# Sparse attention: scores packed in full banks, values and row sums as separate narrow matmuls

## The chip, the cores and the metric

The kernel runs on one core of one Trainium2 chip. The metric is the device time of one execution in microseconds (us), the median of several runs. A core has TensorE (PE in the profile, with its weight loads as PEld), VectorE (DVE), ScalarE (ACT), GpSimd (POOL) and SyncE (SP, which here issues DMAs), each with a queue worked off in order.

## The reference, cut to what matters

The program is a transformer of several layers on 512 tokens of width 1024. The change is in one part of it, the sparse attention of the second block: 16 query heads of 64 in 8 pairs, three branches a head (compressed keys; two branches over all 512 keys with a causal mask, which is what selection and window come to at this length), each with a softmax of its own, then a gate for each branch:

```python
s = einsum('q d, k d -> q k', q, k) * HEAD_DIM**-0.5
p = softmax(where(kpos <= qpos, s, -inf))        # per head and branch
o[b] = p @ v
out = g[0] * o[0] + g[1] * o[1] + g[2] * o[2]    # then @ w_out
```

## The kernel before, in words

The stage works with keys on partitions and queries along the row ("turned"). A pair p has 18 steps (STEPS, lines 139 and 140): for six BLOCKS (branch, half of the pair) one step for the compressed branch 0 and four steps (key tiles kt 0 to 3 of 128 keys, SEQ - 128 kt = 512, 384, 256, 128 queries) for branches 1 and 2. All queues are written out by hand; there is no planner.

- TensorE, `scores_turned`: two matmuls for the keys' high part and for the low part with the maxima (fp32r, L1743 and L1745), and between them a 128x128 causal square (L1744), into bank 0 or 2. Step i waits for the exponential of step i - 2.
- ScalarE, `exps`: the exponential of a step's bank into one of four homes PT (L2697); it waits until the value matmul of four steps before is done.
- TensorE, `outputs_turned`: three steps later (LAG) the value matmul of plain fp32 (L1774). Its 128 stationary columns are 64 of values and 64 of ones, in the order that puts the head's output into its half of the bank and the row sums into the other.
- ScalarE, `keep_outputs`: copies each finished bank; an odd head's copy and its sum are two instructions (L2719, L2723). SyncE sends each sum row to 16 partitions (L934), one transfer after the other.
- Beside it the maxima of the next pair: `find_max` (16 matmuls a pair of 512 to 128 columns, L1700, three banks) and `find_cmp_max` (L1713) on TensorE, `read_max` and `read_cmp_max` on VectorE, `turn_max` (L1721) and `max_to_rows`.
- The pair before is finished meanwhile: `shares` (gate over sum) on VectorE, two transfers by `shares_back`, `spread_share` (L1790) on TensorE, `weigh_parts` (three products, two adds) and `output_low` on VectorE, `output_parts` on ScalarE. The output projection follows (`late_chunks`, L1084); the last pair's spreads stand between its units.

The order of TensorE's queue is the loop behind `rope_part(11, 6, KC)`: scores, then maxima, then spreads, then values, in each step.

Of the kernel before, what the change touches and what calls it, by code (L numbers as in the profile page):

```python
# [19 lines left out]
ALU = mybir.AluOpType  # L20
# [118 lines left out]
BLOCKS = [(0, 0), (1, 0), (0, 1), (1, 1), (2, 0), (2, 1)]  # L139
STEPS = [(_x, _kt) for _x, (_b, _half) in enumerate(BLOCKS) for _kt in range(QT if _b else 1)]  # L140
LAST = [max(_i for _i, (_y, _kt) in enumerate(STEPS) if _y == _x) for _x in range(len(BLOCKS))]
MAXES = [(_t, _half, _b) for _t in reversed(range(QT)) for _half in range(2) for _b in (1, 2)]
N_STEPS, N_BLOCKS, N_MAXES = len(STEPS), len(BLOCKS), len(MAXES)
FINDS = [(0,), (1, 2), (3,), (4,), (5, 6), (7,), (8,), (9,), (10,), (11, 12, 13), (14, 15)]
FIRST_FINDS = [(), (2, 3), ()] + FINDS[3:]
LAG = 3
STACK = 4
TURN_AT, SPREADS_AT, ROWS_AT = 12, (11, 13, 14), (14, 15)
# [135 lines left out]
def build(nc, stream, experts, x_in, vecs_in, consts_in, invcnt_in, iota_in, out):  # L284
    with ExitStack() as ctx:
# [44 lines left out]
        WALK = sb("cell_walk", [P, 2, CELLS + 1], mybir.dt.int32)  # L330
        o_bytes, end_bytes = C * T1 * 4, 2 * FC * SEQ * 4 - C * T1 * 4
# [150 lines left out]
        PT = placed("probs_turned", x_at + 16 * KB, [P, 4, SEQ])  # L482
# [4 lines left out]
        PTR = placed("probs_turned_hi", x_at + 16 * KB, [P, 4, SEQ], F32R)  # L487
# [4 lines left out]
        ODDSUM = placed("odd_sums", ev_at + 12 * KB, [P, SEQ])  # L492
# [273 lines left out]
        def max_bank(n, x):  # L766
            return PS[:, (1, 3, 5, 7)[x % 4] if n == 0 else (1, 3, 7)[x % 3], :]
# [4 lines left out]
        def out_bank(p, x):  # L772
            return PS[:, (4, 6)[x % 2] if p + 1 < PAIRS2 else (4, 7, 6)[x % 3], :]

        def spread_bank(p, b):
            return PS[:, (5, 1, 3)[b], :]

        def o_part(p, b):
            return OP[:, BRANCHES * ((p + 1) % 2) + b, :]
# [48 lines left out]
        def _(sp):  # L828
# [96 lines left out]

            for p in range(PAIRS2):
                for x, (b, half) in enumerate(BLOCKS):
                    done = N_BLOCKS * p + x

                    sp.wait_ge(o_kept, done + 1)  # L930
                    if done:

                        sp.wait_ge(sum_moved, 16 * done)
                    sp.dma_start(SUMP[pieces(half, b), p % 2, :], ODDSUM[0:1, :] if half else o_part(p, b)[HD:HD + 1, :]).then_inc(sum_moved, 16)  # L934
                    if p and x == 0:
                        shares_back(p - 1)
# [57 lines left out]
        def _(pool):  # L994
# [34 lines left out]
            pool.memset(CHOOSE[:, :, :].bitcast(F32), 0.0).then_inc(forms_set, 1)  # L1029

# [43 lines left out]
        def _(pe):  # L1074
# [604 lines left out]
            def find_max(n, x):  # L1679

                t, half, b = MAXES[x]

                pe.wait_ge(qs_ready, 2 * n + half + 1)
                if n == 0 and x == 2:

                    pe.wait_ge(cmax_read, 1)
                if n == 0 and x >= 4:

                    pe.wait_ge(max_read, x - 3)
                if n:  # L1690

                    pe.wait_ge(max_read, N_MAXES * n + max(x - 2, 0))
                    if x == 2:

                        pe.wait_ge(max_rows, 2 * n)
                    if n > 2 and x < 2:

                        pe.wait_ge(part_ready, BRANCHES * (n - 2) - 1 + x)
                g = 2 * (n // 4) + half
                pe.matmul(max_bank(n, x)[:, 0:P * (t + 1)], QS[n][half][:, P * t:P * (t + 1)], KS1[:, b - 1, g, 0:P * (t + 1)],  # L1700
                          start=True, stop=True).then_inc(max_done, 1)

            def find_cmp_max(n):

                pe.wait_ge(qs_ready, 2 * n + 2)
                if n > 2:

                    pe.wait_ge(part_ready, BRANCHES * (n - 2) - 2)
# [7 lines left out]
            def turn_max(n):  # L1716

                pe.wait_ge(max_read, N_MAXES * (n + 1))
                pe.wait_ge(cmax_read, n + 1)
                for t in range(QT):  # L1720
                    mm = pe.transpose(PS[:, 7, t * P:(t + 1) * P], MAXT[:, t, :], ident)  # L1721
                mm.then_inc(max_turned, 1)

            def scores_turned(p, i):

                x, kt = STEPS[i]
                b, half = BLOCKS[x]
# [7 lines left out]
                q0, s = P * kt, score_bank(i)  # L1735
                qs, qm = QS[p][half][:, q0:SEQ], QM[p][half][:, q0:SEQ]
                if b == 0:
                    first, second = (k[:, half, p // 4, :, :].rearrange("p b n -> p (b n)") for k in (KC1, KC2))
                    pe.matmul(s, first, qs, start=True, stop=False, skip_group_check=True)
                    pe.matmul(s, second, qm, start=False, stop=True, skip_group_check=True).then_inc(st_done, 1)  # L1740
                    return
                g = 2 * (p // 4) + half
                pe.matmul(s[:, 0:SEQ - q0], KS1[:, b - 1, g, q0:q0 + P], qs, start=True, stop=False, skip_group_check=True)  # L1743
                pe.matmul(s[:, 0:P], CAUR[:, :], IDA[:, :], start=False, stop=False, skip_group_check=True)  # L1744
                pe.matmul(s[:, 0:SEQ - q0], KS2[:, b - 1, g, q0:q0 + P], qm, start=False, stop=True, skip_group_check=True).then_inc(st_done, 1)  # L1745

            def outputs_turned(p, i):

                x, kt = STEPS[i]
                b, half = BLOCKS[x]  # L1750
                done = N_BLOCKS * p + x

                if b == 0:
                    pe.wait_ge(cmp_low, 2 * p + half + 1)
                else:
                    pe.wait_ge(exp_done, N_STEPS * p + i + 1)
                if p == 0 and x == 0:

                    pe.wait_ge(ones_set, 5)
                if kt == 0 and p + 1 == PAIRS2 and x == 1:  # L1760

                    pe.wait_ge(max_rows, 2 * PAIRS2)
                elif kt == 0 and p + 1 == PAIRS2 and x > 1:

                    pe.wait_ge(o_kept, done - 2)
                elif kt == 0 and done >= 2:

                    pe.wait_ge(o_kept, done - 1)
                probs = PT[:, (N_STEPS * p + i) % 4, 0:SEQ - P * kt]
                if b == 0:  # L1770
                    mm = pe.matmul(out_bank(p, x)[:, :], VCS[:, p // 4, half * HD:half * HD + P], PTR[:, (N_STEPS * p + i) % 4, :], start=True, stop=True,
                                   skip_group_check=True)
                else:
                    mm = pe.matmul(out_bank(p, x)[:, P * kt:SEQ], VV[:, b - 1, p // 4, kt, half * HD:half * HD + P], probs, start=kt == 0,  # L1774
                                   stop=kt == QT - 1, skip_group_check=True)
                mm.then_inc(pv_done, 1)

            def spread_share(p, b):

                pe.wait_ge(share_moved, 32 * (p + 1))  # L1780
                if p and b == 0:

                    pe.wait_ge(part_ready, BRANCHES * p)
                if b == 0:

                    pe.wait_ge(cmax_read, min(p + 3, PAIRS2))
                else:

                    pe.wait_ge(max_read, N_MAXES * min(p + 3, PAIRS2))
# [27 lines left out]
            first_maxima(8, 12)  # L1817
            rope_part(10, 4, KC)
            first_maxima(12, N_MAXES)
# [10 lines left out]
            for p in range(PAIRS2):  # L1830
                for i in range(N_STEPS):
                    scores_turned(p, i)
                    if p + 1 < PAIRS2:
                        if p and i == 0:
                            find_cmp_max(p + 1)
                        for x in (FINDS if p else FIRST_FINDS)[i] if i < len(FINDS) else ():
# [3 lines left out]
                    if p and i in SPREADS_AT:  # L1840
                        spread_share(p - 1, SPREADS_AT.index(i))
                    if i >= LAG:
                        outputs_turned(p, i - LAG)
                    elif p:
                        outputs_turned(p - 1, N_STEPS + i - LAG)
            for i in range(N_STEPS - LAG, N_STEPS):
                outputs_turned(PAIRS2 - 1, i)

            def late_chunks(c, first, last):

                n, r = U["wo2"] + c, R["wo2"] + c
                if r % PAIRS >= 2:

                    pe.wait_ge(o_kept, PAIRS2 * N_BLOCKS)
# [10 lines left out]
            for c in range(AHEAD, C):  # L1865
                n, r = U["wo2"] + c, R["wo2"] + c
                pe.wait_ge(o_kept, PAIRS2 * N_BLOCKS)
# [157 lines left out]
        def _(act):  # L2025
# [615 lines left out]
            def max_to_rows(n, half):  # L2641

                act.wait_ge(max_turned, n + 1)
                act.activation(QM[n][half][other_rows(half), :], PS[other_rows(half), 7, :], ACT.Copy, scale=-1.0).then_inc(max_rows, 1)
# [34 lines left out]
            def exps(p, i):  # L2679

                x, kt = STEPS[i]
                step = N_STEPS * p + i
                b, half = BLOCKS[x]
                width = SEQ - P * kt

                act.wait_ge(st_done, step + 1)
                if step >= 4:

                    act.wait_ge(pv_done, step - 3)
                if b == 0:  # L2690
                    act.activation(PTR[:, step % 4, :], score_bank(i), ACT.Exp)
                    if p or half:

                        act.wait_ge(cmp_low, 2 * p + half)
                    act.activation(CEX[HD:P, :], score_bank(i)[HD:P, :], ACT.Exp).then_inc(exp_done, 1)
                    return
                act.activation(PT[:, step % 4, 0:width], score_bank(i)[:, 0:width], ACT.Exp).then_inc(exp_done, 1)  # L2697

            def keep_outputs(p, x):

                b, half = BLOCKS[x]
# [1611 lines left out]
```

## Time and profile before

| | |
|---|---|
| median of 3 runs | 1941.61 us (1941.1 to 1942.29) |
| profiled execution, its own time | 1941.49 us |
| its span | 1939.7 us |
| PE / PEld busy | 1919.9 us (99%) / 1559.4 us (80%) |
| DVE / ACT / POOL busy | 1385.9 us (71%) / 975.8 us (50%) / 28.7 us (1%) |
| costliest group of the stage | L1774, 256 records, 90.9 us |

The span runs from the first to the last instruction. Busy is the time in which an engine has an instruction in work; matmuls are pipelined, so the lengths of their records overlap, and only the pieces of the chain of waits add up.

### The profile page before, as it was taken

The numbers are of one execution on the slowest core, as the hardware profiler recorded it, in microseconds if no ns is written. First come the engines' busy times: TensorE is split into PE (matmuls) and PEld (weight loads), VectorE is DVE, ScalarE is ACT, GpSimd is POOL, SyncE is SP. The second block draws the span as 40 slices with busy tenths as digits, with TensorE's granted clock in tenths as the row PEclk, the third lists the DMA queues.
The fourth block names the chain that finished last, engine by engine and source line by source line (L and its number), as shares of the span: only waits on it lengthen the run. The fifth ranks groups of instructions, "written<-read, shape, count | busy, mean of one in ns | idle before, by whom it ended". The sixth has DMA issues, their size and how long they took to land.

```text
span 1939.7 us, 26815 instructions
## 1 busy us (share of the span) xinstructions
PE 1919.9 (99%) x9038; PEld 1559.4 (80%) x9038; DVE 1385.9 (71%) x2195; ACT 975.8 (50%) x1422; POOL 28.7 (1%) x50
## 2 busy tenths in 40 slices
PE   9999999999999999999999999999999999999998
PEld 9987888887777788878778888888886788888887
DVE  7986444566999875867746888863388778888534
ACT  5656433446778533677765333333366543333322
POOL 0000000001000000000000000000011000000000
PEclk9999999999999999999999999999999999999999
DMA  5220333326999435400003333333341133333332
GB/s 193 88 66 12 98 97 97 97 94 224 359 350 357 168 89 159 135 23 3 3 6 116 97 95 94 95 103 100 108 123 47 46 97 97 97 97 96 99 108 88
DMA packets 69115, 219.41 MB, mean 113 GB/s; under 512 B 12128, under 2 KB 15360, under 8 KB 68896
## 3 DMA queue, kind: packets, MB, share of 16 engines
q1 hardware_dynamic: 64720, 212.46, 33.7%
q10 hardware_dynamic: 4304, 5.77, 1.2%
q8 instruction: 53, 0.87, 0.2%
q14 instruction: 38, 0.31, 0.1%
HBM read 209.05 MB, written 2.10 MB: 109 GB/s over the span
## 4 chain that ended last, share of the span: by engine, by line
PE 90%; DVE 6%; ACT 2%; issue 1%; DMA 0%; ACTq 0%; SPq 0%; DVEq 0%
PE psum L1084 61%; PE psum L1580 7%; PE psum L1774 3%; PE psum L1554 2%; PE psum L1599 1%; PE psum L1491 1%; PE psum L1563 1%; PE psum L1745 1%; PE psum L1252 1%; PE psum L1700 1%; PE psum L1924 1%; PE psum L1743 1%; PE psum L1634 1%; DVE w_lo L2944 1%; DVE sig L3219 1%
## 5 line engine op out<-in xcount | busy, mean ns | idle before, releaser
L1084 PE MATMUL psum<-x_hi,w_hi 128*128 128x512 f32 (+1 forms) x1344 | 494.1, 378 | 0.0
L1084 PE MATMUL psum<-x_hi,w_lo 128*128 128x512 f32 (+1 forms) x1344 | 490.1, 375 | 0.0
L1084 PE MATMUL psum<-x_lo,w_hi 128*128 128x512 f32 (+1 forms) x1344 | 490.0, 375 | 0.0
L2944 DVE TENSOR_TENSOR w_lo<-raw,w_hi 128x1024 fp32r<-128x1024 f32 x243 | 296.3, 1220 | 187.5 <-ACT w_hi L2046 187.1
L2046 ACT ACTIVATE w_hi<-raw 128x1024 fp32r<-128x1024 f32 x243 | 256.2, 1055 | 190.2 <-DMA raw<-stream 189.5
L1084 PEld LDWEIGHTS psum<-x_hi,w_hi 128*128 128x128 f32 x1344 | 246.5, 188 | 47.3 <-issue 1.9
L1084 PEld LDWEIGHTS psum<-x_lo,w_hi 128*128 128x128 f32 x1344 | 246.5, 188 | 46.5 <-issue 1.4
L1084 PEld LDWEIGHTS psum<-x_hi,w_lo 128*128 128x128 f32 x1344 | 246.4, 188 | 45.5
L1084 PE MATMUL psum<-hid_hi,w_hi 128*128 128x512 f32 (+2 forms) x710 | 261.0, 375 | 0.5 <-DVE hid_lo L4126 0.5
L1084 PE MATMUL psum<-hid_hi,w_lo 128*128 128x512 f32 (+2 forms) x710 | 259.7, 373 | 0.0
L1084 PE MATMUL psum<-hid_lo,w_hi 128*128 128x512 f32 (+2 forms) x710 | 259.6, 373 | 0.0
L2063 ACT ACTIVATE staged<-psum 128x512 f32<-128x512 f32 (+1 forms) x116 | 69.1, 595 | 216.6 <-PE psum L1084 202.4
L1084 PEld LDWEIGHTS psum<-hid_hi,w_hi 128*128 128x128 f32 x710 | 131.4, 188 | 25.4 <-issue 1.1
L1084 PEld LDWEIGHTS psum<-hid_hi,w_lo 128*128 128x128 f32 x710 | 131.3, 188 | 23.5
L1084 PEld LDWEIGHTS psum<-hid_lo,w_hi 128*128 128x128 f32 x710 | 131.3, 188 | 23.5 <-issue 0.2
L2169 ACT ACTIVATE squares<-squares 128x512 f32<-128x512 f32 x44 | 27.9, 633 | 215.0 <-DVE squares L3095 215.0
L1774 PE MATMUL psum<-probs_turned,values_and_ones 128*128 128x512 f32 (+3 forms) x256 | 90.9, 438 | 0.0
L3035 DVE TENSOR_TENSOR resid<-resid,staged 128x512 f32<-128x512 f32 x39 | 26.9, 689 | 79.3 <-ACT staged L2063 77.4
L2931 DVE TENSOR_TENSOR w_lo_more<-raw_more,w_hi_more 128x1024 fp32r<-128x1024 f32 x56 | 67.0, 1212 | 12.1 <-ACT w_hi_more L2033 12.1
L3821 DVE CUSTOM_DVE_ANT_0 psum<-psum,causal_mask 128x512 f32<-128x512 f32 (+3 forms) x128 | 60.3, 514 | 12.2 <-PE psum L1700 11.7
L2931 DVE TENSOR_TENSOR w_lo<-raw,w_hi 128x1024 fp32r<-128x1024 f32 x57 | 68.1, 1211 | 0.7 <-ACT w_hi L2033 0.7
L2697 ACT ACTIVATE probs_turned<-psum 128x512 f32<-128x512 f32 (+3 forms) x128 | 55.0, 431 | 25.9 <-PE psum L1745 24.4
(651 smaller groups left out, 2966.6 us busy)
## 6 DMA issues: line engine op xcount, KB each, us to landing
raw<-stream SPq DMA_DIRECT2D x251, 512.0 KB, 3.6
raw<-experts SPq DMA_DIRECT2D x70, 512.0 KB, 5.3
raw_more<-experts SPq DMA_DIRECT2D x68, 512.0 KB, 5.3
staged<-staged ACTq DMA_DIRECT2D x64, 64.0 KB, 3.2
out_fm<-resid SPq DMA_DIRECT2D x7, 256.0 KB, 2.2
resid<-x_fm SPq DMA_DIRECT2D x3, 528.0 KB, 7.3
consts<-consts_in SPq DMA_DIRECT2D x1, 1373.0 KB, 14.1
staged<-staged SPq DMA_DIRECT2D x20, 64.0 KB, 2.7
```

The lines of the kernel that those rows point to most:

```text
L1084: last = pe.matmul(o, wt[:, slot, k * P:(k + 1) * P], m[part], start=start and p == 0, stop=stop and p == 2, skip_group_check=True)
L1554: mm = pe.matmul(pair(r)[:, half, :], HT[:, b, :] if m % M_OUT == 0 else HTW[:, :], moe_slot("raw", s)[:, half * 512:(half + 1) * 512], st ...
L1580: mm = pe.matmul(pair(r)[:, 0, :], x[:, part, f * P:(f + 1) * P], moe_slot(kind, s)[:, k * 512:(k + 1) * 512], start=f == 0 and p == 0, st ...
L1774: mm = pe.matmul(out_bank(p, x)[:, P * kt:SEQ], VV[:, b - 1, p // 4, kt, half * HD:half * HD + P], probs, start=kt == 0, stop=kt == QT - 1 ...
L2046: act.activation(w_hi[:, slot, :], raw[:, slot, :], ACT.Copy).then_inc(hi_split, 1)
L2063: act.activation(shaped(dst, t), result(rslot, t), func, **more).then_inc(lin_free, 1)
L2169: act.activation(SQ[:, j, 0:T2], SQ[:, j, 0:T2], ACT.Silu).then_inc(act_done, 1)
L2697: act.activation(PT[:, step % 4, 0:width], score_bank(i)[:, 0:width], ACT.Exp).then_inc(exp_done, 1)
L2931: dve.tensor_tensor(moe_slot("lo", s), moe_slot("raw", s), moe_slot("hi", s).bitcast(F32), ALU.subtract).then_inc(m_ready, 1)
L2944: dve.tensor_tensor(w_lo[:, slot, :], raw[:, slot, :], w_hi[:, slot, :].bitcast(F32), ALU.subtract)\
L3035: dve.tensor_tensor(h, h, staged(E0[name] + c, t), ALU.add).then_inc(ev_used, 1)
L3821: dve.tensor_tensor_reduce(out=s, in0=s, in1=AFTER[:, SEQ - width:], scale=1.0, scalar=NEG, op0=ALU.add, op1=ALU.max, accum_out=MAXT[:, t, ...
```

## The change

A pair has 12 steps, each a full bank of 512 columns: two for the compressed branch, four for key tile 0, four that hold key tile 1 (384) and key tile 3 (128) of one branch and head, two that hold key tile 2 (256) of both heads. Two parts in a bank share one causal matmul of 256 columns. Maxima of query tile 1 take both branches in one matmul, those of tile 0 lie four in a bank; their banks are two instead of three. Probabilities have eight homes. Values are computed in three bursts a pair (`values_side_by_side`): key tile 0 after step 8, tiles 3 and 1 after step 11, tile 2 in step 1 of the next pair. Each value matmul has 64 stationary columns, and the two heads of a branch go to partitions 0 to 63 and 64 to 127 of one bank; the sums are matmuls of their own with 32 columns of ones, four to a bank. ScalarE keeps two full banks and one bank of sums; the sums go out in four transfers at once. The two adds a pair go to GpSimd (all but the last pair's), and the third spread and product of a pair move to the pair after the next.

```diff
+STEPS = [[(0, _half, 0, 0)] for _half in range(2)] + [[(_b, _half, 0, 0)] for _b, _half in ROW] \
+    + [[(_b, _half, 1, 0), (_b, _half, 3, SEQ - P)] for _b, _half in ROW] + [[(_b, _half, 2, SEQ // 2 * _half) for _half in range(2)] for _b in (1, 2)]
+VALUES = [[0], [3, 1], [2]]
+SLOTS_PT, STACK = 8, 4
+FINDS = [(), (0,), (1,), (2, 3), (4,), (5, 6), (7,), (8,), (9,), (10,), (), ()]
+CMP_AT, TURN_AT, ROWS_AT = 1, 10, (10, 11)
+CMP_OUT_AT, VALUES_AT = (3, 4), (8, 11, 1)
+SPREADS_AT, LAST_SPREADS_AT = (10, 11, 0), (8, 9, 10)
...
+            def sums_out(p):
+                sp.wait_ge(o_kept, N_KEPT * (p + 1))
...
+                for x, (b, half) in enumerate(ROW):
+                    sp.dma_start(SUMP[pieces(half, b), p % 2, :], SUMR[32 * x:32 * x + 1, :]).then_inc(sum_moved, 16)
...
+            def add_parts(p):
+                for b in (1, 2):
+                    pool.wait_ge(part_ready, BRANCHES * p + b + 1)
...
+                    pool.tensor_tensor(o_part(p, 0), o_part(p, 0), o_part(p, b), ALU.add).then_inc(parts_added, 1)
...
+                    pe.wait_ge(max_read, N_MAXES * n + max(x - 1, 0))
...
+                for x, (b, half, kt, col) in enumerate(STEPS[i]):
+                    pe.matmul(s[:, col:col + SEQ - P * kt], KS1[...], QS[p][half][:, P * kt:SEQ], start=x == 0, stop=False, ...)
+                if len(STEPS[i]) == 1:
+                    pe.matmul(s[:, 0:P], CAUR[:, :], IDA[:, :], ...)
                 else:
+                    squares = s.rearrange("p (c n) -> p c n", n=P)[:, 0:QT:STEPS[i][1][3] // P, :]
+                    pe.matmul(squares, CAUR[:, :], IDA[:, :].unsqueeze(1).to_broadcast([P, 2, P]), ...)
...
+            def values_side_by_side(p, x):
+                pe.wait_ge(exp_done, N_STEPS * p + VALUES_NEED[x])
...
+                for b in (1, 2):
+                    for kt in VALUES[x]:
+                        for half in range(2):
+                            i, col = PLACE[b, half, kt]
+                            pe.matmul(values_bank(b)[half * HD:(half + 1) * HD, P * kt:SEQ], VV[:, b - 1, p // 4, kt, 2 * half * HD:(2 * half + 1) * HD],
+                                      PT[slot_of(p, i)][:, col:col + SEQ - P * kt], start=kt == 0, stop=kt == 2, skip_group_check=True)
+                for kt in VALUES[x]:
+                    for row, (b, half) in enumerate(ROW):
+                        i, col = PLACE[b, half, kt]
+                        mm = pe.matmul(sums_bank()[32 * row:32 * row + 32, P * kt:SEQ], VV[:, b - 1, p // 4, kt, HD:HD + 32],
+                                       PT[slot_of(p, i)][:, col:col + SEQ - P * kt], start=kt == 0, stop=kt == 2, skip_group_check=True)
+                mm.then_inc(pv_done, 1)
...
             for p in range(PAIRS2):
                 for i in range(N_STEPS):
                     scores_turned(p, i)
+                    if i == SPREADS_AT[2] and 2 <= p:
+                        spread_share(p - 2, 2)
+                    if i == VALUES_AT[2] and p:
+                        values_side_by_side(p - 1, 2)
                     if p + 1 < PAIRS2:
+                        if p and i == CMP_AT:
                             find_cmp_max(p + 1)
+                        for x in (FINDS if p else FIRST_FINDS)[i]:
                             find_max(p + 1, x)
                         if i == TURN_AT:
                             turn_max(p + 1)
+                    if i in CMP_OUT_AT:
+                        cmp_outputs(p, CMP_OUT_AT.index(i))
...
+                    if i in VALUES_AT[0:2]:
+                        values_side_by_side(p, VALUES_AT.index(i))
...
 # ScalarE, in each step after exps(p, i)
+                    if p and i in (1, 2):
+                        keep_values(p - 1, i)
+                    if p and i == 3:
+                        keep_sums(p - 1)
+                    if i == 4:
+                        keep_cmp(p, 0)
+                    if i == 5 and p + 2 < PAIRS2:
                         queries_high(p + 2)
+                    if i == 6:
+                        keep_cmp(p, 1)
+                    if i == 7 and p > 1:
+                        output_parts(p - 2)
...
 # VectorE, in each pair
                 if p > 1:
+                    weigh_part(p - 2, 2)
+                cmp_probs_low(p, 0)
                 if p and p + 1 < PAIRS2:
                     read_cmp_max(p + 1)
                     read_max(p + 1, 0)
+                    read_max(p + 1, 1)
...
+                cmp_probs_low(p, 1)
...
+                    for x in range(2, 7):
+                        read_max(p + 1, x)
                 if p:
                     shares(p - 1)
                 if p + 1 < PAIRS2:
+                    for x in range(7, N_MAXES):
                         read_max(p + 1, x)
```

## Rows read from the trace of the kernel before

**Rows 1.** The page: busy time by engine, and the chain by engine.

```profile
PE 1919.9 (99%) x9038; PEld 1559.4 (80%) x9038; DVE 1385.9 (71%) x2195; ACT 975.8 (50%) x1422; POOL 28.7 (1%) x50
PE 90%; DVE 6%; ACT 2%; issue 1%; DMA 0%; ACTq 0%; SPq 0%; DVEq 0%
```

**Rows 2.** Stretches: us, busy of PE, PEld, DVE, ACT, POOL, clock, DMA, GB/s.

```profile
828.80:1000.70 171.90, 170.77 (x896) 133.71 (x895) 120.50 (x342) 137.11 (x280) 0.89 (x2) 1.00 0.04 8
...
893.96:915.83 21.87, 21.87 (x120) 17.46 (x119) 16.31 (x49) 17.67 (x36) 0.00 (x0) 1.00 0.02 2
```

**Rows 3.** The chain of waits over one pair, 893.6 to 915.45: start, us, piece.

```profile
by line: PE psum L1774 40.4%; PE psum L1745 14.6%; PE psum L1700 13.7%; PE psum L1743 10.7%; PE psum L1744 5.3%; PE psum L1713 3.6%; PE psum L1790 3.4%; PE psum L1739 3.1%; PE psum L1740 2.1%; PE psum L1771 2.1%; PE psum L1721 2.0%
...
894.00 0.80 PE psum L1713 x8
...
895.12 0.65 PE psum L1774 x2
895.76 0.23 PE psum L1743
895.99 0.06 PE psum L1744
896.05 0.29 PE psum L1745
...
897.94 0.22 PE psum L1774 x2
...
898.92 0.06 PE psum L1743
898.98 0.11 PE psum L1744
899.09 0.11 PE psum L1745
...
904.89 0.48 PE psum L1700 x3
905.37 0.93 PE psum L1774 x2
```

**Rows 4.** The chain at matmuls of small shapes: fox values, compressed values.

```profile
138.57 0.32 PE psum L1252 x2
138.89 0.32 PE psum L1236
...
755.99 1.02 PE psum L1675 x16
757.00 1.12 PE psum L1084 x4
```

**Rows 5.** ScalarE's groups, 850 to 980 us: busy, mean ns; idle before, releaser.

```profile
L2697 ACT ACTIVATE probs_turned<-psum 128x512 f32<-128x512 f32 x24 | 14.4, 598 | 11.2 <-PE psum L1745 10.9
...
L2723 ACT ACTIVATE odd_sums<-psum 1x512 f32<-1x512 f32 x18 | 10.6, 587 | 0.2
L2715 ACT ACTIVATE o_parts<-psum 128x512 f32<-128x512 f32 x18 | 10.5, 584 | 0.0
```

**Rows 6.** VectorE's groups, 850 to 980 us, and GpSimd's, whole span.

```profile
L3821 DVE CUSTOM_DVE_ANT_0 psum<-psum,causal_mask 128x512 f32<-128x512 f32 x24 | 16.4, 704 | 0.2
...
L3897 DVE TENSOR_TENSOR o_parts<-o_parts 128x512 f32<-128x512 f32 x12 | 8.3, 692 | 0.4
...
L3872 DVE RECIPROCAL gate_over_sum<-sum_pieces 96x32 f32<-96x32 f32 x6 | 2.1, 344 | 0.0
...
L1024 POOL TENSOR_TENSOR cmp_values_stacked<-cmp_values_and_ones,cmp_values_stacked 31x384 fp32r<-31x384 f32 x2 | 2.8, 1380 | 119.7 <-ACT cmp_values_stacked L2668 119.6
```

**Rows 7.** L934, the sums' transfers: issue ns, and time to landing.

```profile
L934 SPq DMA_DIRECT2D sum_pieces<-odd_sums x24: 502/502/565, 841.8 to 1002.4; - x24
...
DMA to landing us min/median/max: 1.6/1.6/3.4
```

More of the change, by code:

```diff
@@ L481, in build @@
         QM = [lo_pair("q_and_max_first", 2)] + [qm_ring[n % 2] for n in range(PAIRS2 - 1)]
-        PT = placed("probs_turned", x_at + 16 * KB, [P, 4, SEQ])
+        homes = [x_at + (16 + 2 * n) * KB for n in range(4)] + [x_at + (32 + 2 * n) * KB for n in range(2)] + [more_at + 2 * n * KB for n in range(2)]
+        PT = [placed(f"probs_turned_{n}", home, [P, SEQ]) for n, home in enumerate(homes)]
         SUMP = placed("sum_pieces", x_at + 24 * KB, [P, 2, PIECE])
@@ L1679, in find_max @@
             def find_max(n, x):
-                t, half, b = MAXES[x]
-                pe.wait_ge(qs_ready, 2 * n + half + 1)
+                t, half, bs = MAXES[x]
+                pe.wait_ge(qs_ready, 2 * n + (1 if half is None else half) + 1)
                 if n == 0 and x == 2:
@@ new lines, in scores_turned, with cmp_outputs @@
+                for b, half, kt, col in STEPS[i]:
+                    mm = pe.matmul(s[:, col:col + SEQ - P * kt], KS2[:, b - 1, 2 * (p // 4) + half, P * kt:P * (kt + 1)], QM[p][half][:, P * kt:SEQ],
+                                   start=False, stop=True, skip_group_check=True)
+                mm.then_inc(st_done, 1)
+            def cmp_outputs(p, half):
+                pe.wait_ge(cmp_low, 2 * p + half + 1)
+                if p == 0 and half == 0:
+                    pe.wait_ge(ones_set, 5)
+                if p:
+                    pe.wait_ge(o_kept, N_KEPT * (p - 1) + 3 + half)
+                pe.matmul(out_bank(half), VCS[:, p // 4, half * HD:half * HD + P], PTR[slot_of(p, half)][:, :], start=True, stop=True,
+                          skip_group_check=True).then_inc(pv_done, 1)
@@ L2679, in exps @@
             def exps(p, i):
-                x, kt = STEPS[i]
                 step = N_STEPS * p + i
-                b, half = BLOCKS[x]
-                width = SEQ - P * kt
                 act.wait_ge(st_done, step + 1)
[L2687 to L2694, printed above, removed]
+                if step >= SLOTS_PT:
+                    q, j = divmod(step - SLOTS_PT, N_STEPS)
+                    act.wait_ge(pv_done, N_OUTS * q + FREES[j])
@@ L3936, in _ @@
                     dve.tensor_tensor(CHOOSE[0:2 * SUMS2, :, :].rearrange("p b (h d) -> p h b d", h=2), hi_rows, lo_rows, ALU.add)
+                elif p + 1 < PAIRS2:
+                    for b in range(2):
+                        weigh_part(p - 1, b)
+                else:
+                    for b in range(BRANCHES):
+                        weigh_part(p - 1, b)
             for n in range(2, AHEAD + 1):
@@ L3940, in _ @@
             shares(PAIRS2 - 1)
-            weigh_parts(PAIRS2 - 1)
+            for b in range(BRANCHES):
+                weigh_part(PAIRS2 - 1, b)
+            add_parts(PAIRS2 - 1)
             output_low(PAIRS2 - 1)
```

296 lines of the change are left out of this document (147 added, 149 removed).

## The prediction

> **What bounds the kernel now.** The page comes first: TensorE is busy for 99% of the span and holds 90% of the chain that ended last [rows 1]. Its stretches come next, at a granted clock of 1.00: the sparse attention lies at 828.8 to 1000.7 us, 171.9 us for eight pairs of heads, and one middle pair takes 21.87 us, in which TensorE is busy for all 21.87, ScalarE for 17.67, VectorE for 16.31 and GpSimd not at all [rows 2]. Then the chain inside a pair, where each piece on TensorE is the time until the next may go: it splits the pair completely [rows 3]. L1774 (values) has 40.4% of it, 8.84 us; the turned scores (L1743 to L1745) 30.6%; the maxima (L1700) 13.7%. The stage is bound by TensorE's columns, with nothing of another engine to be seen between them. What is to be read is therefore how many columns TensorE streams, what short matmuls waste, and whether the new order lets another engine into the chain.
>
> **The values.** A value matmul is plain fp32 and leaves two records: 512 columns take 0.93 us, against 0.23 for a score matmul of 512, so it is four passes, two in each record; 384 take 0.65 and 128 take 0.22 [rows 3]. Before, a pair has 16 of them (4 sets of 512, 384, 256 and 128), 8.84 us. Their 128 stationary columns are 64 of values and 64 of ones. The change issues each twice: with 64 columns of values, the two heads in the two halves of one bank, and with 32 columns of ones, four in the four quarters of another. Nothing in this trace shows two matmuls in different columns of the array at once, so the price is bounded from both sides. If they share no time, 32 matmuls of these lengths cost 2 x 8.84 = 17.68 us. If neighbours run wholly beside each other, two heads cost one and four sums cost one: 8.84/2 + 8.84/4 = 6.63. I take 6.63: the outputs lie in disjoint partitions, the weights in disjoint columns, the order in the code alternates between them, and no data orders them. The Trainium skill, TensorEngine Tiling (Array Packing), Tiling Modes, states that different tiles load weights and multiply in parallel; no run here shows it.
>
> **Changing the shape of the array.** Each of a pair's three bursts of values goes from 128 columns to 64, to 32, and back: 9 changes a pair. The nearest rows are matmuls of small shapes [rows 4]. The fox value of 16 rows and 16 columns takes 0.32 us where its columns need under 0.05, and the 272 columns behind it 0.32 where 272/512 of 0.23 is 0.12: 0.45 for two changes. Sixteen records at L1675, 31 stationary columns and 64 moving, two passes each, take 1.02 where their columns need 16 x 0.23/4 = 0.92 or less, and the four matmuls of 512 behind take 1.12 for 4 x 0.23 = 0.92: about 0.3 for two changes. So a change costs 0.1 to 0.23. The value taken is 0.15 (nearest to L1675, which is narrow in columns as here): 9 x 0.15 = 1.35 a pair, bounds 0.9 and 2.1. The same page of the Trainium skill, Key Properties, says that changing the mode drains TensorE, and the rows agree: 0.3 to 0.45 us for a way in and out.
>
> **Scores and maxima.** Their columns stay the same (5120 twice, 2048 of causal squares, 5120 of maxima). What goes is the wait for weights behind a matmul of 128 columns: the matmul of 512 behind the square takes 0.29 instead of 0.23, and the two behind a short key matmul 0.11 each where 0.06 would do [rows 3]. Steps 1+3 share a square of 256 columns, and so do the two halves of step 2: about 0.07 less for each of 4 double banks and 0.1 for 2, 0.5 a pair. Of the 16 maxima eight short ones become four of 256 and 512 columns: three short ones take 0.48 [rows 3], so 0.25 less. Together 0.75 a pair, bounds 0.4 and 1.0.
>
> **ScalarE, VectorE and GpSimd.** ScalarE evacuates ten full banks (6.0 us at 598 ns) instead of 16 partial ones (6.9), and keeps six outputs instead of nine (about 0.59 each) [rows 5]: 17.7 falls to about 15. VectorE gives two adds of 0.69 a pair to GpSimd; it reads the same columns of maxima. GpSimd's two-input operation of 384 columns takes 1.38 [rows 6], so 1.84 for 512 and 3.7 a pair, beside some 21 us in which it has nothing else: no cost on the path. If it slows VectorE, the whole overlap is 3.7 us a pair and VectorE has over 5 idle; bounds 0 and 0.5.
>
> **The new order puts waits in.** Values now come in three bursts, so between the third burst (in the next pair's second step) and the first burst (ninth step) TensorE does seven steps of scores without values to cover the others: pieces as above give 0.80 (compressed maxima) + 4.4 (scores: four banks at 0.58, three at 0.69) + 1.9 (nine maxima) + 0.46 (two compressed outputs), about 7.5 us up to the tenth maximum. That matmul waits for reads that stand on VectorE behind the shares of the pair before. Those need all six sums: ScalarE reaches the sums after two exponentials and two kept banks, at about 1.8 + 4 x 0.6 = 4.2 us; SyncE then issues four transfers at 0.5, each 1.6 to landing [rows 7], so the last lands at about 7.3; reciprocal and its followers take about 1.0 (0.34 for the first), a read 0.7 [rows 6]: 9.0. The maximum, and the first burst queued behind it, come up to 1.5 us late. ScalarE is a second limit: the ninth scores want the seventh exponential, the last of some ten operations of 0.6 that start at 1.8, so at about 7.8. I take 1.0 for six of the eight pairs (the first has no shares behind it, the last no maxima), bounds 0 and 2.0. Eight homes hide the rest: an exponential wants the home of eight steps before, which the matching burst has left by then.
>
> **Tail.** Before, the chain goes from the values straight into the output projection, and the three spreads at 1010.3 cost 0.2 of waiting. After, the four transfers go together instead of one after another and are as early: 0, bounds -0.5 and 1.5.
>
> **The sum.** A pair: values 6.63 - 8.84 = -2.21; changes +1.35; short matmuls -0.75: -1.61. Eight pairs: -12.9; stalls 6 x 1.0 = +6: -6.9 us. The profiled run before took 1941.49, 1.8 more than its span of 1939.7 and 0.1 under the median of 1941.61. That gives 1934.6, told as 1935. This case's own range: cheap changes (0.9), best savings (1.0) and no stall give 8 x -2.31 = -18, so 1923; dear ones (2.1, 0.4, 2.0 in six pairs) 8 x 0.29 + 12 = +14, which I don't expect together: 1947.
>
> **Rivals.**
> - **Two records in order (slower).** Each fp32 value matmul is two records on the same columns of the array. If matmuls start in the order issued, the second record of one waits for its first, and only this second record can run beside the next matmul's first. Then every matmul costs one record's time whether two or four stand side by side: 32 x half of before = 8.84 a pair, plus the first record of each of six groups alone (0.47, 0.06 and 0.22, twice, about 1.5): 10.3 instead of 6.63, 3.7 more, 8 x 3.7 = 30: 1965. For it: the two records that each L1774 row counts. Against: nothing here. It decides whenever a queued record blocks the one behind it. TensorE: Matmul & The Clock Gate (the Trainium skill), Part 3, has matmuls start and end strictly in program order, which is this mechanism; no run here shows it yet. Between (half of the overlap lost) lies 1950.
> - **No overlap at all.** 17.68 instead of 6.63: 8 x 11.05 = 88 us: 2023. Against: the disjoint columns. It is also the case in which the change doesn't do what it says.
> - **Overlap, but the stalls eat it (no change).** Changes at 0.2 (+0.45 a pair) and stalls of 1.5 (+0.5 in six): +6.6 on 1935: 1941. For: the walk above gave up to 1.5. Against: the kept slack of 5 us on both engines.
> - **Overlap and free stalls.** 1923, as above.
>
> **Chances.** Overlap as forecast or better 0.47 (1923 to 1937); overlap with stalls 0.13 (1937 to 1947); records in order 0.30 (1950 to 1975); none 0.10. About 0.2% (3.9 us) is what a measurement of this kernel can tell from no change. Faster by more 0.46, within it 0.13, slower 0.41. The range, 1921 to 1968, takes in all but the worst of the third case and the fourth.
>
> **What would show it.** Right: in the chain, values plus sums near 6.6 us a pair, a pair of 20.3 us, and idle time before the tenth maximum released by VectorE. Value records of both heads starting together would show overlap; starts one whole record apart would show the order rival; sums as dear as values would too. GpSimd at 3.7 us a pair, beside an unchanged VectorE row. Wrong: a pair over 22 us with TensorE never idle (order, or no overlap), or TensorE idle over 2 us a pair.

## The result and the profile after

The changed kernel takes 1966.18 us (median of 4 runs, 1962.33 to 1972.3) against 1941.45 (1941.1 to 1942.29) of the kernel before on the same chip: a ratio of 1.0119, interval 1.0099 to 1.0138. It is slower by 1.2%. The forecast was 1935, and 1966 lies inside the range only because the order rival (1965) widened it. As will be seen, that rival's mechanism is not what happened. Some executions of several kernels here, the one before too, take 5 to 6 us longer than the rest (in the profiled ones of e3, e7 and e7b TensorE ran at half clock for 13.65 us from 411 us on, far ahead of the sparse attention), which lifts the median of e7b, where half of them do, by some 2 us.

The page of the kernel after, busy time by engine and the chain by engine (against [rows 1]):

```profile
PE 1919.4 (98%) x9214; PEld 1531.2 (78%) x9214; DVE 1382.1 (70%) x2181; ACT 956.2 (49%) x1350; POOL 47.4 (2%) x64
PE 89%; DVE 5%; ACT 2%; DMA 1%; issue 1%; SPq 1%; DVEq 0%; ACTq 0%
```

TensorE's busy time is the same 1919 us although the values should have become cheaper, and DMA and SyncE's queue have entered the chain with 1% each, 10 to 29 us apiece (the page rounds). Where the sparse attention ends tells where all of it lies: 1000.72 us before, 1024.37 after, which is 23.65 later, and the span grew by 23.6. Stretches of the kernel after (columns as in [rows 2]): the whole stage to 1026, then ten us and ten more in its last pair.

```profile
828.80:1026.00 197.20, 171.27 (x1078) 106.07 (x1079) 115.26 (x325) 118.03 (x208) 18.67 (x14) 0.96 0.03 7
1003.00:1013.00 10.00, 3.15 (x15) 1.84 (x15) 2.28 (x6) 3.93 (x7) 0.00 (x0) 0.70 0.03 4
1013.00:1023.00 10.00, 10.00 (x67) 4.28 (x65) 4.34 (x4) 2.52 (x4) 3.36 (x2) 0.78 0.00 0
```

Reading the start of each pair's compressed scores in both traces gives the account of the 23.65 us: 0.8 before the second pair, then 1.3, 1.7, 1.7, 1.7, 4.3 and 1.7 for six middle pairs, and 10.5 for the last. A quiet middle pair, one at a granted clock of 1.00 throughout, takes 23.54 us (897.30 to 920.84) against 21.87, and TensorE is busy for 21.37 of it where before it never stopped [rows 2]. The pair with 4.3 (944.38 to 970.61) is not quiet: the landing of its sums takes 2.78 us instead of 1.73, and its first burst 3.55 instead of 1.94, with the clock at half for 3.41 us from 959.31.

The chain inside that pair, against [rows 3], up to and through its first burst, then its second and third:

```profile
902.67 0.35 ACT o_parts L2790
...
903.15 0.60 ACT probs_turned L2762
903.75 0.50 ACT sum_rows L2798
...
904.27 0.57 SPq L957
...
904.89 0.58 SPq L957
...
905.52 0.58 SPq L957
...
906.14 1.73 DMA sum_pieces<-sum_rows
...
907.89 0.02 SPq L964
...
907.94 1.64 DMA sum_pieces<-o_parts
...
909.66 0.35 ACT o_parts L2778
...
910.27 0.60 ACT cmp_probs_turned L2779
910.86 0.14 issue
911.00 1.94 PE psum L1831 x8
912.93 1.00 PE psum L1836 x8
913.93 0.43 PE psum L1797 x2
...
916.26 0.65 PE psum L1777 x4
...
917.97 1.88 PE psum L1831 x16
919.84 1.00 PE psum L1836 x16
...
922.20 1.01 PE psum L1831 x8
923.22 0.57 PE psum L1836 x8
```

Two things are to be seen. The bursts (the three groups of value and sum matmuls of a pair) are cheap: L1831 (values) and L1836 (sums) take 2.94 + 2.88 + 1.58 = 7.40 us a pair where L1774 took 8.84. And ahead of the first one stands a chain without TensorE: ScalarE keeps the four sums (L2798), SyncE issues their transfers (L957), the last one lands, only then (L964) does SyncE send the compressed sum of the even head, that lands, ScalarE may overwrite its source (L2778, L2779), and only then may the burst overwrite the bank they were read from. In the last pair the same chain is followed by the shares on their way back (L948, then the spread L1852), and by a slow burst:

```profile
1006.92 0.60 ACT cmp_probs_turned L2779
...
1007.54 0.50 SPq L965
...
1008.14 0.78 SPq L948
...
1008.96 2.07 DMA share_rows<-gate_over_sum_parts
...
1011.07 0.80 PE psum L1852
1011.87 3.61 PE psum L1831 x8
1015.48 1.87 PE psum L1836 x8
```

The burst that took 1.94 + 1.00 takes 3.61 + 1.87: half speed, the lower of the clock's two levels (1.2 GHz), granted from 1007.09 to 1017.33. From 1003.07 to 1011.07, ahead of the burst, TensorE had been busy for 1.16 of 8 us. The shares' way back is not new in this place. The last pair of the kernel before has it too, with TensorE busy for 6.57 of the 6.75 us from 985.63 to 992.38:

```profile
989.41 0.78 SPq L924
...
990.24 2.10 DMA share_rows<-gate_over_sum_parts
```

### The profile page after: what moved, and what is told of

Its sections match the earlier page's. It is cut to its first block, busy times and chain, and to the rows that moved or that the text cites. A ratio compares the mean times of both kernels' runs of the same rounds, so it can differ in the third digit from the quotient of the medians.

```text
span 1963.3 us, 26958 instructions
## 1 busy us (share of the span) xinstructions
PE 1919.4 (98%) x9214; PEld 1531.2 (78%) x9214; DVE 1382.1 (70%) x2181; ACT 956.2 (49%) x1350; POOL 47.4 (2%) x64
## 4 chain that ended last, share of the span: by engine, by line
PE 89%; DVE 5%; ACT 2%; DMA 1%; issue 1%; SPq 1%; DVEq 0%; ACTq 0%
PE psum L1134 63%; PE psum L1630 6%; PE psum L1604 2%; PE psum L1831 2%; PE psum L1649 1%; PE psum L1541 1%; PE psum L1613 1%; PE psum L1302 1%; PE psum L1836 1%; PE psum L1991 1%; PE psum L1684 1%; DVE sig L3300 1%; DVE psum L4102 1%; DVE psum L3905 1%; DMA sum_pieces<-sum_rows 0%
## 5 line engine op out<-in xcount | busy, mean ns | idle before, releaser
L3905 DVE CUSTOM_DVE_ANT_0 psum<-psum,causal_mask 128x512 f32<-128x512 f32 (+3 forms) x128 | 60.1, 514 | 33.7 <-PE psum L1752 29.8
L2762 ACT ACTIVATE probs_turned<-psum 128x512 f32<-128x512 f32 x80 | 47.3, 594 | 38.0 <-PE psum L1805 36.9
L3170 DVE TENSOR_TENSOR staged<-psum,scratch 128x512 f32<-128x512 f32 x88 | 60.3, 686 | 5.8 <-PE psum L1134 4.8
```

What stands on the lines that cost most here:

```text
L2762: act.activation(PT[slot_of(p, i)][:, :], score_bank(i), ACT.Exp).then_inc(exp_done, 1)
L3170: dve.tensor_tensor(EV[:, slot, 2:2 + T2], PS[:, 2 * ((r0 + m) % PAIRS), :], TS[:, 2, 0:T2], ALU.mult)\
L3905: ins = dve.tensor_tensor_reduce(out=s, in0=s, in1=AFTER[:, SEQ - width:], scale=1.0, scalar=NEG, op0=ALU.add, op1=ALU.max, accum_out=MAXT ...
```

## Experiments

Lines are two lower from e1 on, except in g1, which has the changed kernel's, and p1 and e6, where some differ again: L1829 and L1834 are the changed kernel's L1831 and L1836, L1748 and L1750 its L1750 and L1752, L1767 its L1769, L3903 its L3905. All are timed beside the kernel before on the same chip (its medians: 1941.91 for the first four, 1942.11 for the next four, 1941.75 for the three after, 1941.63 for the last). A ratio is not exactly the quotient of the two medians. A pair's length is that of a middle pair in the chain of the profiled execution.

**The compressed sums counted by themselves (e1).** The even head's compressed sum waited for the landing of the four other sums only because all six share one semaphore.

```
-  sp.wait_ge(sum_moved, 16 * (N_SUMS * p + half))       # behind the four others
+  sp.wait_ge(gates_moved, 16 * (PAIRS2 + 2 * p + half)) # a count of its own
```

> The changed kernel with one edit: the transfers of the compressed sums are counted on a count of their own, so that the even head's compressed sum no longer waits until the four sums of the pair before have landed. Theory A (waits): the value bursts overlap fully and cost 7.4 us a pair, and the time is lost before the first burst of each pair, in a chain sums kept, four issues, landing (1.73), compressed sum, landing (1.64), odd output kept. One landing leaves the chain; then the shares on VectorE (behind the same landing, about 1.0, and a read of 0.7) are late next, so about 1.1 of the 1.7 comes back in seven pairs: 8 us less than the changed kernel, about 1958. Theory B (shape of the array): narrow matmuls and the changes between them cost what the pair lost, and the waits only fill it: no change, 1966.

1957.09 us, ratio 1.0096 (1.0067 to 1.0125), a pair of 22.86 us. The landing left the chain and 9.5 us came back by the medians (each against the kernel before beside it), 7.8 between the two profiled executions, so this chain was real. It held 0.7 us in most pairs, 2.0 of the last pair (28.18 us for 30.20), and the 2.7 us that one pair lost more than the others. What stands ahead of the first burst in e1's middle pairs is VectorE's reads and split and ScalarE's copies of the queries, not the shares, which I had expected next.

**Compressed output kept and sent ahead of the sums (e2 = e1 and this; SyncE's order and count follow).**

```
-  if p and i == 3: keep_sums(p - 1)
-  if i == 4: keep_cmp(p, 0)
+  if i == 3: keep_cmp(p, 0)
+  if p and i == 3: keep_sums(p - 1)
```

> As e1_own_count, and the even head's compressed output is kept, and its sum sent, before the four sums of the pair before. Theory A: the whole chain over the compressed sum is gone, but the tenth maximum still stands behind the shares, so little more than e1_own_count comes back: 1953 to 1958. Theory B: no change, 1966. If theory A is right but the shares are not the next limit, 1945.

1963.51, ratio 1.0120 (1.0103 to 1.0137), a pair of 23.9: worse than e1, against my expectation. In its chain the sums are kept at 905.55, their last transfer lands at 910.66, and the shares and the reads queued behind them on VectorE hold the maxima. That is the stall that the prediction had walked, at last in the place it was given.

**Shares later on VectorE (e3 = e2 and this)**: two more reads of maxima ahead of them, the last pair's spreads a step later, the split of the odd compressed probabilities ahead of the two weight splits.

```
-  for x in range(2, 7): read_max(p + 1, x)
+  for x in range(2, 9): read_max(p + 1, x)
   shares(p - 1)
-  LAST_SPREADS_AT = (8, 9, 10)
+  LAST_SPREADS_AT = (9, 10, 11)
```

> As e2_cmp_first, and on VectorE two more reads of maxima stand ahead of the shares of the pair before; in the last pair the three spreads are one step later (behind the first burst), and the odd compressed probabilities are split before the two weight splits. Theory A: the first burst then waits only for ScalarE's exponentials, 2.3 us a pair earlier than in the changed kernel, and the last pair, which waited some 7 us for its shares, loses about 4: 1942 to 1947. Theory B: 1966 less the last pair's wait, about 1960.

1951.21, ratio 1.0048 (1.0031 to 1.0065), a pair of 22.86: 12 us better than e2 and still short of what I expected; ahead of the turned maxima (L1775) four reads of VectorE stood in the chain. The middle pair is only back at e1's 22.86; against e1 the 6 us are those of the last pair (22.04 us for 28.18).

**The last maxima a step earlier (e4 = e3 and this).**

```
-  FINDS = [..., (8,), (9,), (10,), (), ()]
+  FINDS = [..., (8,), (9, 10), (), (), ()]
```

> As e3_shares_later, and the last group of maxima (four short reads on VectorE, 1.2 us, for which the turning of the maxima waited) is computed one step earlier, ahead of the first burst. Theory A: this 1.2 us a pair hides beside the burst: 8 us less than e3_shares_later, 1934 to 1939, which would be under the kernel before (1941.5). Theory B: no change against e3_shares_later.

1944.38, ratio 1.0016 (1.0006 to 1.0026), a pair of 21.85. That is 6.8 us less than e3 where I expected 8, and outside the 1934 to 1939 that I had counted from a better e3. The wait before the turn has gone. Of the 24.7 us of loss, 22 are undone by one count and the order of the work, without touching the bursts.

**Order of issue, and twice as many changes of shape (g1 = the changed kernel and this)**: first burst head by head, second burst in four parts instead of two.

```
-  x == 0: for b: for half: matmul          # even, odd, even, odd
+  x == 0: for half: for b: matmul          # even, even, odd, odd
-  x == 1: values of blocks 3, 1; sums of blocks 3, 1
+  x == 1: values of 3; sums of 3; values of 1; sums of 1
```

> The changed kernel with two edits inside its bursts. First burst (key tile 0): the two value matmuls of the even heads, then the two of the odd heads, instead of alternating. If TensorE starts matmuls strictly in the order issued and each waits for its own columns, only the second and third can share time: 3 lengths of 0.86 instead of 2, so about 2.8 us instead of 1.94. If each set of columns has a queue of its own, 1.94 as before. Second burst: values of key tile 3, its sums, values of tile 1, its sums, so that the array's shape changes four times inside it instead of once and twice at its ends as before, two changes more. By my price (0.15 a change) the burst grows by 0.3 from 2.88 us; by the rival's (the changes are what the time went to) by 0.5 or more.

1963.16 in its one run. The chain of g1, first burst and second:

```profile
887.08 1.94 PE psum L1831 x8
889.03 1.00 PE psum L1836 x8
...
894.07 0.59 PE psum L1831 x8
894.65 0.36 PE psum L1836 x8
895.01 1.44 PE psum L1831 x8
896.45 0.78 PE psum L1836 x8
```

The first burst takes 1.94 and 1.00 in either order: two matmuls of the same columns in a row do not keep the other columns waiting. (A record doesn't say which columns it ran on; the burst's length and the records' starts, two at a time in both orders, say this.) The second takes 3.17 in four parts where it took 2.88 in two: 0.29 for two more changes, 0.15 each.

**The adds back on VectorE (p1 = e4 and this).**

```
-  pool: add_parts(p)        # two adds a pair
+  dve:  add_parts(p - 2), add_parts(p - 1) behind their products
```

> e4_maxima_earlier with the two adds of a pair back on VectorE, ahead of the compressed probabilities of the pair after the next. If GpSimd's adds cost nothing there, VectorE's 1.4 us stand in the chain that now ends the waits (maxima read, then found): up to 1.4 us in each of six pairs slower, 1949 to 1953 against 1944. If instead GpSimd's adds slowed VectorE beside them, no change or up to 3 us faster.

1944.08, ratio 1.0007 (0.9994 to 1.0020): the same as e4. The groups of 850 to 980 us show what GpSimd's adds do to VectorE; first the changed kernel (e4's mean is 1065), then p1 (the split of the compressed probabilities):

```profile
L3968 DVE TENSOR_TENSOR probs_turned_hi<-cmp_probs_turned,probs_turned_hi 64x512 fp32r<-64x512 f32 x12 | 12.8, 1066 | 5.8 <-ACT cmp_probs_turned L2760 5.7
```

```profile
L3965 DVE TENSOR_TENSOR probs_turned_hi<-cmp_probs_turned,probs_turned_hi 64x512 fp32r<-64x512 f32 x12 | 8.3, 689 | 7.2 <-ACT cmp_probs_turned L2756 6.9
```

Five of the twelve splits in this stretch run beside an add and take 1.59 or 1.60 us, the others 0.69, which makes the mean of 1066 ns: 0.9 us that VectorE loses in a pair, against 1.4 us of adds that it is spared.

**ScalarE's copies moved beside the bursts (e5 = e4 and this)**: the copy of the next queries from step 5 to 8, the odd compressed output from step 4 to 5, the second split behind two more reads.

```
-  if i == 5 and p + 2 < PAIRS2: queries_high(p + 2)
+  if i == 8 and p + 2 < PAIRS2: queries_high(p + 2)
-  CMP_OUT_AT = (3, 4)
+  CMP_OUT_AT = (3, 5)
```

> e4_maxima_earlier with ScalarE's two copies of the queries (0.63 each) after the ninth exponential, beside the first burst, instead of after the sixth, and VectorE's split of the odd compressed probabilities after the fourth read instead of after the second (its compressed output one step later). What is left in e4's chain before the first burst is VectorE's read and split (0.7 each) and ScalarE's copies, about 3 us of waits a pair. Theory A: 1.0 to 1.5 us of them go in six or seven pairs: 1935 to 1938, faster than the kernel before (1941.9). Theory B (full pairs are at TensorE's limit already): no change, 1944.

1944.27, ratio 1.0015 (1.0001 to 1.0028), the pair unchanged at 21.85: no gain, where I expected 6 to 9 us. ScalarE has left the chain, and what stands there instead is one engine, from the end of the compressed maxima's matmuls (L1767) to the fifth maximum. Chain of e5:

```profile
896.01 1.01 PE psum L1767 x8
...
897.04 0.43 DVE psum L3887
...
897.84 0.69 DVE psum L3903
...
900.67 0.69 DVE probs_turned_hi L3967
...
901.39 0.57 DVE psum L3903
...
902.21 0.41 PE psum L1748
```

VectorE's 5.2 us between 897.04 and 902.21 cannot start before the third burst and the compressed maxima are over: TensorE's chain of 16.6 and VectorE's of 5.2 make 21.8.

**The last pair's spreads behind its second burst (e6 = e5 and this).**

```
-  if p + 1 == PAIRS2 and i in LAST_SPREADS_AT: spread_share(p - 1, ...)   # before the burst
+  if p + 1 == PAIRS2 and i == N_STEPS - 1: all three spreads              # behind it
```

> As e5_copies_in_burst, and in the last pair all three spreads stand behind the second burst, since they waited 3 us for the shares' landing ahead of it. Theory A: about 2 us less, 1933 to 1936, unless the output projection then waits for the next to last pair's output (up to 1.5 us given back).

1944.68, ratio 1.0009 (0.9995 to 1.0024), no gain either. The burst no longer waits for the shares, but the products and the splits of the output weights now stand in the chain ahead of the output projection (3.7 us of L3024). The wait moved by one place.

**The third burst behind the maxima (e7 = e5 and this; e7b = e4 and this; e8 = e5 with it one step later still).**

```
-  step 1: scores, values(p - 1, 2), find_cmp_max, find 0
+  step 1: scores, find_cmp_max, find 0, values(p - 1, 2)
```

> e5 with the third burst of values (block kt=2, 1.6 us) issued after the compressed maxima and the first maxima matmul of the same step instead of ahead of them. In e5's trace VectorE stands in the chain from 897.04 to 902.21 (5.2 us: compressed maxima and five reads), and TensorE waits about 1.2 us in it for banks of maxima; the burst ends just ahead of it. Theory A (that chain of reads, begun behind the burst, is what holds e5 at the old 21.85 us a pair): the burst now lies beside the reads, the waits go, a pair takes 20.7 us, six pairs gain 1.1 each: 1937 us (1935 to 1940), under the kernel before. Rival B (the wait only moves: values are kept 1 us later, or the bank of the compressed maxima is not free yet because the third spread and its product stand in front): pair 21.8, 1944. Rival C (TensorE's own work fills the pair, records hide it): no change, 1944.

> As e7, but the third burst one step later still, behind the second maxima matmul of step 2, and ScalarE keeps the values one step later each (steps 2 and 3). Theory A: the reads' chain starts as early as in e7 and the burst sits in the middle of it, where e5's TensorE idles longest: 1936 (1934 to 1940). Rival B (values and sums are kept 1 us later, the transfers and the compressed probabilities behind them on ScalarE too): a wait ahead of the first burst of each pair, 1942 to 1950.

> The same edit as e7 on e4 (without e5's three moves). It tells whether e5's moves, worth nothing by themselves (1944.27 against 1944.38), matter once the maxima start earlier. Theory A: 1937 to 1941, no better than e7. If e5's moves are worth nothing in any case, both are equal; if e4 had a wait behind the reads (ScalarE's copy of the queries ahead of the odd compressed output), e7b stays 2 to 4 us above e7.

In the order of these texts, 1945.83 (e7; ratio 1.0026, 1.0015 to 1.0037), 1946.12 (e8; 1.0022, 1.0014 to 1.0031) and 1947.89 (e7b; 1.0027, 1.0016 to 1.0038): in all three theory A missed, by 6 to 7 us beyond its upper bound. The pair did not get shorter but longer, 22.25 in e7. In its chain the compressed maxima wait 0.86 us for the last product of the pair before, and behind the burst the third maximum is only issued at 905.03, so VectorE's reads begin again from there: 3.5 us of VectorE in a pair of 22.25.

**The whole chain of maxima earlier (e9 = e7 and this).**

```
-  FINDS = [(), (0,), (1,), (2, 3), (4,), (5, 6), (7,), ...]
+  FINDS = [(), (0, 1), (2,), (3, 4), (5,), (6,), (7,), ...]
-  step 0: scores, spread(p - 2, 2)
+  step 0: spread(p - 2, 2), scores
```

> e7 left the third maxima matmul where it was (step 3, 905.03 in its trace), behind the burst that it had put in front: VectorE read two maxima by then and waited, so the four reads and the split of 2.1 us stood in the chain after all, and the compressed maxima waited 0.84 us for the last product of the pair before. Here the maxima matmuls come one step earlier each (two of them beside the compressed maxima), and the third spread goes ahead of the compressed scores. Theory A (what keeps every rearrangement at the old 21.85 us a pair is VectorE's serial chain: compressed maxima, reads, split): with the chain begun earlier and the burst beside it a pair takes 20.8 to 21.2 us, 1938 us (1935 to 1941). Rival B (VectorE is late again in another place, since its product for the third spread now stands in front of the first split): 1943 to 1948.

1941.38 us, ratio 0.9996 (0.9986 to 1.0006): 3 us short of the 1938 that I expected, the best order found, and level with the kernel before. Its chain over the same part of the pair, and the stretch that holds five pairs and more:

```profile
894.69 0.97 PE psum L1767 x8
895.65 0.56 PE psum L1748 x2
896.22 1.01 PE psum L1829 x8
897.23 0.57 PE psum L1834 x8
...
901.17 0.57 DVE psum L3903
```

```profile
850.00:980.00 130.00, 126.90 (x856) 81.46 (x854) 89.08 (x273) 90.14 (x161) 14.02 (x12) 1.00 0.02 3
```

The burst lies beside VectorE's reads and one read is left in the chain. A pair takes 21.37 us, and adding up the chain's pieces over one (893.75 to 915.12) gives TensorE 20.28, VectorE 0.66 and 0.42 of issue. What this saves in six pairs (3.2 us) is given back at the ends. The second pair starts 1.3 us later than before, and the last takes 21.2 us (979.17 to 1000.36), 1.5 more than the last before: ahead of the shares' way back, which stood in the chain before too, the copy of the four sums, their issue and their landing stand in it now (984.85 to 989.31). The late start goes with the clock. In the first pair of e9, as of every kernel here with the new order except g1, TensorE runs at half clock for 3.41 us, which before it didn't; the stretch 828 to 836 ahead of it, in which it was busy for 3.38 of 8 us, had 7.70 before:

```profile
828.00:836.00 8.00, 3.38 (x15) 1.95 (x13) 6.13 (x14) 3.95 (x7) 0.85 (x2) 1.00 0.40 106
836.49:839.90 3.41, 3.41 (x12) 3.02 (x12) 1.36 (x6) 1.50 (x3) 0.00 (x0) 0.50 0.08 15
```

Half of 3.41 is 1.7, an estimate of what this costs, and enough for the 1.3.

## Why the prediction was wrong

- **Full overlap: right.** Two heads cost one, four sums cost one. Less the changes of shape, the first burst's four values cost 2 x 0.93 = 1.86 [rows 3] where the sets' rows show 1.94, and its four sums 0.93 where they show 1.00. In the trace the first two value records start within 0.01 us of each other at 911.00, and the first four of the sums within 0.02 at 912.86; g1 shows that the order of issue does not matter. The order rival (1965) and the one without overlap (2023) are wrong, the first in spite of its number.
- **0.15 us a change of shape: right.** g1 gives 0.29 for two. In the chain part of the cost sits in the piece behind each burst (L1797: 0.43 at 913.93, where undisturbed 384 and 128 columns take 0.23), so reading the bursts alone understates it: 7.33 in them and 3 x 0.2 behind make 7.93 a pair in e9, 1.30 over full overlap, for which the prediction had 1.35.
- **TensorE's own sum, -1.61 us a pair: right.** It asked for a pair of 20.3 us. e9's chain has 20.28 on TensorE against 21.87 before, -1.59. Less the 7.93 of values and 8.84 before, that leaves -0.68 for the short matmuls, for which the prediction had -0.75.
- **"Up to 1.5 us late", 1.0 taken, 2.0 the bound: this step failed.** The changed kernel loses 23.54 - 20.28 = 3.26 us in a quiet middle pair. The walk followed the four sums through the shares to the tenth maximum. Its times were good: it had the last sum land 7.3 us behind the third burst, the trace has 7.6 (900.24 to 907.88). But the path that it followed from there isn't in the chain. It left out that SyncE sends the compressed sum behind the same count, so behind the landing of the four (two transfers in a row, 1.73 and 1.64), that ScalarE's two copies of the odd compressed output wait for that, and that the first burst wants their bank. e1, which takes that one wait away, gives 9.5 us back. The walked stall itself shows only in e2, whose order makes it, and goes again in e3. The 13 us from e1 to e4 are the last pair's (6) and, at 1.0 us in each middle pair, four reads ahead of the turned maxima.
- **A second limit was not seen at all.** The prediction walked TensorE's steps against ScalarE and SyncE, and took VectorE's 5 idle us a pair for slack. But the compressed maxima, five reads and a split (5.2 us) are a serial chain. It starts when the third burst is over, and at its end TensorE waits for a bank to hold its next maximum. With the old values TensorE had enough to do meanwhile. That is why e5 stands at 21.85 us although TensorE's own work is 20.3 (in e4 ScalarE's copies of the queries stood in the chain too, behind three of these reads and the split). Only e9, which starts that chain ahead of the burst and has each maximum ready for it, comes under it.
- **Tail 0, bounds -0.5 and 1.5: wrong.** The last pair costs 10.5 us more. The same chain stands in it, and behind it the shares' way back (2.9 us from L948's issue to the spread), which the kernel before had under cover of a busy TensorE. From 995.49 to 1011.07 TensorE is busy for only 7.68 of 15.58 us, and then its burst runs at half clock for 5.5 us: 3.61 + 1.87 instead of 1.94 + 1.00 is 2.5 us. The prediction had neither this wait nor the lower clock.
- **GpSimd: right in effect.** Its adds take 1.28 to 1.36 us on average against the forecast 1.84, and slow one split a pair by 0.9 us; p1 finds no time in it.
- **One bound of the range was added up wrongly.** The dear end, changes 2.1, savings 0.4 and stalls 2.0 in six pairs, is 8 x (-2.21 + 2.10 - 0.40) + 12 = +8, so 1950; the prediction has 0.29 for the bracket and +14. Nothing in the result hangs on it: with the stalls at their bound of 2.0 a pair would still have been 1.3 us short of the measured 3.26.

The account: six middle pairs at -1.6 + 3.3, the first of them 0.4 better and the fifth 2.7 worse (landing and clock), make 12.4, the start 0.8, the last pair 10.5: 23.7 us. TensorE's saving of 12.7 (8 x 1.59) was there the whole time; the waits that the new order made, with the lower clock behind them, cost 36 us, nearly three times as much. That 1966 lies next to the order rival's 1965 is chance.

What stays open: whether the first pair can be ordered so that TensorE keeps its clock, and the last so that it keeps its 19.7 us; then a pair of 21.37 would be worth 3 us. A third bank for maxima, which might take VectorE out of the chain, was not tried.

## What to carry to other kernels

When one engine's work shrinks inside a stage that it alone filled, list every cycle of waits that runs once round the loop (engine, queue, landing, shared counter) with its length, before adding up the saving: here the pair stood at 23.54 us, at 22.86 when the first wait had gone and at 21.85 when the next had, and the saving of 1.6 was not to be seen behind any of them. Follow a wait through each thing that shares its semaphore, for a count that mixes two sources makes the second wait for the first's landing. And where TensorE would be mostly idle for several us, price the next burst at half speed as one of the outcomes: here it came behind 1.16 us of work in 8 (1003.07 to 1011.07), and not behind 6.43 in 8 (903.00 to 911.00). Between these it went either way: it came behind 5.75 in 8 (951.13 to 959.13), and not in g1 behind 5.00 in 8 (828 to 836).

## What the hardware showed

- fp32 matmuls on 64 of the array's columns ran wholly beside those on the other 64, and on 32 columns four at a time: 1.94 us for four of 512 columns and 1.00 for four sums, against 0.93 for one alone [rows 3]. Two in a row on the same columns did not block the others (g1).
- A change between shapes cost 0.15 us (g1), and the first score behind a burst took 0.2 more than elsewhere (0.43 for 0.23).
- Behind a stretch in which it was busy for 1.16 of 8 us, TensorE ran a burst for 5.5 us at half speed (1.2 of 2.4 GHz): 3.61 us for values that take 1.94.
- A GpSimd add of 128x512 (1.28 us) stretched a VectorE subtraction of 64x512 from 0.69 to 1.60 us where it lay beside the add for 1.05 us, and to 0.89 in e9, where it lay beside it for 0.34. No read of a maximum lay beside an add between 850 and 1000 us, so nothing is shown for those.
